# Keep-warm matmuls around TensorE's second modulation slab, and the first parts of x ahead of weight casts, in a two-block transformer kernel

## The reference, cut to what matters

```python
cs = silu(c)                              # c: 1 x 1024
mod = cs @ w_ada[l] + b_ada[l]            # w_ada: 1024 x 6144
sh_a, sc_a, gt_a, sh_f, sc_f, gt_f = split(mod, 6)
h = rms_norm(x, g_mix[l]) * (1 + sc_a) + sh_a
u = h @ w_in[l]                           # w_in: 1024 x 9728
rq, rk, rv, rg, aq, ak, av, ga, gb = split(u, pts)
```

## Time and profile before

| | us |
|---|---|
| median of 3 executions | 1921.5 (1921.12 to 1921.51) |
| span of the profiled execution | 1919.6 |
| TensorE busy | 1826.0 (95%) |
| VectorE busy | 785.6 (41%) |
| ScalarE busy | 570.1 (30%) |
| mean DMA rate | 309 GB/s |

### The profile page before, as it was taken

How to read it: one execution, slowest core, us unless ns; L and a number is a source line. 1 busy time by engine, 2 the same in 40 slices (tenths; PEclk the granted TensorE clock), 3 DMA queues, 4 the chain that set the end, 5 groups by cost and what they waited for, 6 DMA issues and landing times. The chain is left out here.

```text
span 1919.6 us, 24342 instructions
## 1 busy us (share of the span) xinstructions
PE 1826.0 (95%) x9814; PEld 1167.5 (61%) x9814; DVE 785.6 (41%) x1150; ACT 570.1 (30%) x911; POOL 17.0 (1%) x33
## 2 busy tenths in 40 slices
PE   7999999999999999999999999999999999999998
PEld 6799888743333333333333333337888888878886
DVE  6867655411111111111111111115676656666665
ACT  4444554310101000001010010004555544545552
POOL 1000001000000000000000000000000000000000
PEclk7999999999999999999999999999999999999999
DMA  9976756599999999999999999997456646336552
GB/s 343 323 251 230 243 176 217 208 429 428 431 431 430 430 430 431 429 432 431 429 431 431 431 430 430 430 420 233 132 176 197 187 165 219 111 110 198 184 178 99
DMA packets 155400, 592.36 MB, mean 309 GB/s; under 512 B 6703, under 2 KB 85743, under 8 KB 128832
## 3 DMA queue, kind: packets, MB, share of 16 engines
q1 hardware_dynamic: 152816, 582.90, 77.3%
q0 software_dynamic: 2512, 8.45, 1.4%
HBM read 590.26 MB, written 1.07 MB: 308 GB/s over the span
## 5 line engine op out<-in xcount | busy, mean ns | idle before, releaser
L1674 PE MATMUL psum<-shared,expert_arena 128*64 128x512 f32 x1536 | 341.5, 596 | 23.0 <-DMA shared<-in_w_mlp_dram 23.0
L1533 DVE TENSOR_SCALAR expert_arena<-psum 128x512 f32<-128x512 f32 x32 | 22.1, 692 | 583.7 <-PE psum L1674 583.7
L1674 PEld LDWEIGHTS psum<-shared,expert_arena 128*64 128x64 f32 x1536 | 105.5, 137 | 242.5 <-issue 198.8
L415 PE MATMUL psum<-layer_x_parts,layer_w_hi 128*128 128x512 f32 x704 | 240.5, 396 | 0.4 <-DVE layer_x_parts L2144 0.4
L1439 ACT ACTIVATE expert_arena<-expert_arena 128x512 f32<-128x512 f32 x32 | 20.1, 629 | 562.5 <-DVE expert_arena L1533 562.5
L414 PE MATMUL psum<-layer_x_parts,layer_w_lo 128*128 128x256 f32 x616 | 171.8, 279 | 0.0
L352 DVE TENSOR_TENSOR mixer_w_lo<-mixer_ring,mixer_w_hi 128x1024 fp32r<-128x1024 f32 x96 | 116.4, 1223 | 96.7 <-ACT mixer_w_hi L347 96.4
L352 DVE TENSOR_TENSOR layer_w_lo<-slots_ahead,layer_w_hi 128x1024 fp32r<-128x1024 f32 x96 | 116.9, 1224 | 94.5 <-ACT layer_w_hi L347 94.5
L347 ACT CAST mixer_w_hi<-mixer_ring 128x1024 fp32r<-128x1024 f32 x96 | 100.0, 1048 | 158.1 <-PE psum L385 94.2
L415 PEld LDWEIGHTS psum<-layer_x_parts,layer_w_hi 128*128 128x128 f32 x704 | 125.8, 188 | 24.6 <-DVE layer_x_parts L2144 0.8
L383 PE MATMUL psum<-layer_w_hi,layer_x_parts 128*128 128x512 f32 (+1 forms) x384 | 138.7, 361 | 0.4 <-DVE layer_x_parts L2144 0.4
(11 more groups left out here) (311 smaller groups left out, 2683.0 us busy)
## 6 DMA issues: line engine op xcount, KB each, us to landing
shared<-in_w_mlp_dram SPq DMA_DIRECT2D x98, 2048.0 KB, 22.0
expert_ring<-in_w_mlp_dram SPq DMA_DIRECT2D x64, 2048.0 KB, 25.4
mixer_ring<-in_w_in_dram SPq DMA_DIRECT2D x38, 1024.0 KB, 6.3
slots_ahead<-in_w_mlp_dram SPq DMA_DIRECT2D x15, 2048.0 KB, 25.7
mixer_ring<-in_w_ada_dram SPq DMA_DIRECT2D x22, 1024.0 KB, 6.2
slots_ahead<-in_w_ffn_in_dram SPq DMA_DIRECT2D x21, 1024.0 KB, 4.9
memory_kv<-in_w_mlp_dram SPq DMA_DIRECT2D x15, 1024.0 KB, 24.7
kept<-in_w_mlp_dram SPq DMA_DIRECT2D x15, 1024.0 KB, 26.7
```

The source lines that it names most:

```text
L415: last = self.nc.tensor.matmul(out, hi, both[:, k].rearrange("p h s -> p (h s)"), start=k == 0, stop=k == KC - 1)
L1533: nc.vector.tensor_scalar(glu, both[:, :, 0], LIMIT, None, ALU.min).then_inc(glu_ready, 1)
L1674: last = nc.tensor.matmul(U[CAP * h:CAP * h + CAP, N * n:N * n + N], xg[:, k, j, :], expert_slot(M, k // 2)[:, at:at + N], start=False, st ...
```

## The change

TensorE gets keep-warm matmuls: 7 after the scale's slab and before it waits for the shift's slab, one more ahead of columns 2 and 5 of that slab, and 5 between `col1` and `col0a`. ScalarE computes the high parts 0 and 1 of h before the cast of unit 1 (so far after it). VectorE no longer splits unit 0 before `col0a`: it does so within it, after the values 0 and 1, and then forms the low parts 0 and 1, the values 2 and 3, their low parts and unit 1's.

```diff
+            def first_highs(part):
+                act.wait_ge(freed_by_act, jobs.by_name["nT11"].freed)
+                act.wait_ge(scale_ready, 1)
+                wait_freed(act, "col0a" if part[0] < 4 else "col0b")
+                for k in part:
+                    nc.scalar.activation(xh[:, k, :], nT[:, k, :], ACT.Identity, bias=shift[:, k:k + 1], scale=scale[:, k:k + 1]).then_inc(hx_high, 1)
                 if what == "split":
+                    if job == 1:
+                        first_highs(range(2))
                     stream.split_high(act, job)
...
                     if name in ("col0a", "col0b"):
-                        act.wait_ge(freed_by_act, jobs.by_name["nT11"].freed)
-                        act.wait_ge(scale_ready, 1)
-                        wait_freed(act, name)
-                        for k in range(4) if name == "col0a" else range(4, KC):
-                            nc.scalar.activation(xh[:, k, :], nT[:, k, :], ACT.Identity, bias=shift[:, k:k + 1], scale=scale[:, k:k + 1]).then_inc(hx_high, 1)
+                        first_highs(range(2, 4) if name == "col0a" else range(4, KC))
...
                     if job == 0:
                         scale_out()
-                    if job != 1:
+                    if job > 1:
                         stream.split_low(dve, job)
...
-                    for k in [*part, None]:
...
-                        if low >= part[0]:
...
+                    for k in part:
+                        value(k)
+                        if k % 4 == 1 and name == "col0a":
+                            stream.split_low(dve, 0)
+                            low_part(0)
+                            low_part(1)
+                        elif k > part[0] and k % 4 != 2 or name == "col0b" and k % 4 == 2:
+                            low_part(k - 1)
+                    low_part(part[-1])
                     if name == "col0a":
                         stream.split_low(dve, 1)
...
+                        if g == 0:
+                            keep_busy(nc, M, spare, 7)
                         stream.wait_here(pe, job.slots[0])
...
                         for k in range(KC):
+                            if g == 0 and k % 3 == 2:
+                                keep_busy(nc, M, spare, 1)
...
                     g = int(name[3])
+                    if name == "col0a":
+                        keep_busy(nc, M, spare, 5)
                     pe.wait_ge(stream.taken, ada_last[g])
```

More of the change, by code:

```diff
@@ L944, in _, with value, low_part @@
                     wait_freed(dve, "nT11")
-                    for k in [*part, None]:
-                        if k is not None:
-                            nc.vector.tensor_scalar(hT[:, k, :], nT[:, k, :], scale[:, k:k + 1], shift[:, k:k + 1], ALU.mult, ALU.add).then_inc(h_value, 1)
-                        low = part[-1] if k is None else k - 1
-                        if low >= part[0]:
-                            dve.wait_ge(h_value, low + 1)
-                            dve.wait_ge(hx_high, low + 1)
-                            nc.vector.tensor_tensor(xl[:, low, :], hT[:, low, :], xh[:, low, :].bitcast(FP32), ALU.subtract).then_inc(hx_low, 1)
+                    def value(k):
+                        nc.vector.tensor_scalar(hT[:, k, :], nT[:, k, :], scale[:, k:k + 1], shift[:, k:k + 1], ALU.mult, ALU.add).then_inc(h_value, 1)
+                    def low_part(k):
+                        dve.wait_ge(h_value, k + 1)
+                        dve.wait_ge(hx_high, k + 1)
+                        nc.vector.tensor_tensor(xl[:, k, :], hT[:, k, :], xh[:, k, :].bitcast(FP32), ALU.subtract).then_inc(hx_low, 1)
+                    for k in part:
[7 more added lines that the diff above has]
+                    low_part(part[-1])
                     if name == "col0a":
```

## The result

The changed kernel is slower. Median of 6 executions 1929.13 us (1923.88 to 1931.62) against 1921.48 (1921.12 to 1923.92) for 6 of the kernel before; ratio 1.0032, 95% interval 1.0021 to 1.0042.

The account below looks back on a forecast made before the run. The start was taken as bound by col0a, VectorE's chain, POOL's tables and the w_ada slab up to unit 12. Gain 2.01 - 1.14 = 0.87; 1919.6 - 0.87 = 1918.7, plus 1.9 gives 1920.6 us; range 1918.6 to 1925.3.

Parts of the forecast that it names:

- C: TensorE, shift's slab and col1: the clock falls again among one-column matmuls; 1925.3 or 1929.5 us; chance 0.18.
- Step (1): TensorE, seven keep-warm matmuls from 20.0: clock back after 1.5 us, so the shift's slab starts at 23.92.
- Steps (2) and (3): TensorE: slab at full clock to 28.55, col1 to 30.42, five keep-warm to 32.68, addition at 33.67; gain 2.01 us.
- Step (4): VectorE's chain: unit 0's low part now stands inside it, 1.14 us lost, leaving 0.87 of the gain.
- Step (5): ScalarE: two high parts before unit 1's cast stay hidden behind VectorE's work and cost nothing.
- The path to unit 12: From col0a through VectorE's chain, POOL's tables, the w_ada slab's landing and VectorE again: only 0.87 us survives at unit 12.
- rival B: DMA: the landings don't move at all, so the chain's 0.87 us is lost too; 1921.5 us; chance 0.12.
- Rival A: The w_ada slab's landing doesn't hold VectorE, so TensorE's 2.7 us at unit 2 stay; 1918.8 us; chance 0.17.

Follow-up runs that it names:

- cold-start variant: Changed against the kernel before: col1 ahead of the shift's slab, new order, many keep-warm matmuls in both slabs, none ahead of the transposes; 1927.55 us, ratio 1.0027.
- late_tables: The kernel before with POOL's three bias table loads issued only after unit 39's low part; 1920.5 us against 1921.85, ratio 0.9993.
- no_five: The changed kernel without the five keep-warm matmuls between col1 and col0a; 1925.79 us, ratio 1.001 against the kernel before.
- col1_only: The kernel before with col1 run ahead of the shift's slab, POOL's tables early as before; 1920.98 us against 1922.22, ratio 0.9995.

## Why the prediction was wrong

The forecast was 1920.6 within 1918.6 to 1925.3; it came out at 1929.1. The case on the other side, C, was named, with 1925.3 or 1929.5 as its times, and given 0.18.

In short, the step that failed is the cost of the keep-warm matmuls: forecast at a clock that comes back after 1.5 us and then holds, they and the one-column matmuls around them ran mostly at the half clock, and the first shift addition came at 42.99 instead of 33.67.

**Step (1) failed first.** "I take 1.5 us, a quarter of that" priced the seven at 3.92 us from 20.0. The profile has 6.0 us from 22.67. Two things are in it. The 1.5 us were too short by themselves: in the five other profiles with the seven, whose first slab was fast, they took 4.6 to 4.8 us. And I had taken the first slab's full clock as given, as the change doesn't touch it. It is not given: of the eleven profiled kernels whose transposes have no keep-warm matmul in front (both originals among them, with the cold-start variant left out), five show about 6.8 us for it and six 3.7 to 3.9. The Trainium skill ("TensorE: Matmul & The Clock Gate", Part 1) says that the number of slow matmuls at a kernel's start differs from run to run; the traces agree, by 3.1 us for this slab. One profiled execution could not show it, and three equal times hid it: in the kernel before an idle gap lies behind this slab, and where it was slow there (`late_tables`) nothing was lost.

**Steps (2) and (3) failed by the same assumption,** a clock that holds through one-column matmuls. Laid end to end against 42.99: start 2.67 later than I had it, the seven 2.07 more, the slab 0.72, `col1` 1.54, the five 2.15, `col0a` 0.17, together 9.3 us after 33.67. The five are the largest mistake in the change itself: 4.4 us on the path in front of `col0a`. C's mechanism was right: in all six profiles with the seven the clock fell again within the second slab or `col1` (27.4 to 32.0). Its chance was too low. That its 1929.5 lies so near 1929.1 is in part luck: C had the clock fall as the slab begins, 4.2 us dearer than forecast for the slab, where the profile lost 0.72 there and 4.7 before it, in step (1), which C had left alone. The rows had already shown the clock falling among one-column matmuls with the engine busy, and nothing showed it held by a few others between them.

**Step (4) was right:** 1.14 forecast, 1.05 measured in the chain.

**Step (5) was right:** no delay by ScalarE's new order shows beyond the 1.05 of step (4), and in the total the order alone has no measurable cost.

**The path to unit 12 was right, its elasticity wrong.** I let the slab's landing move with POOL's issue. It does so when the chain is late: in the changed kernel VectorE got it 8.6 us after its issue at 53.87, as before. Where the chain came 0.92 us earlier (`no_five`), the slab still landed at about 54.2, 9.6 us after its issue, and at 54.0 in `col1_only`, so 0.87 would have shrunk to nothing: rival B, given 0.12. Why an earlier issue doesn't help stays open. And "45.50 + 8.6 meets 54.12 to the hundredth" said more than its rows: the landing is known to 0.1 us, and VectorE had no idle time ahead of that take. Rival A needs the tables out of the way, and then it works in part (unit 12 at 72.37). The rule of the Trainium skill on alternating queues ("DMA: Bandwidth & Descriptors", Queues, rings and completion order) is not borne out by 46 to 48 here. Later in the same trace it agrees: from 50 to 51 SP's queue q1 and POOL's q0 had about half each.

```profile
q1 hardware_dynamic: 41, 0.17, 51.5%
q0 software_dynamic: 42, 0.17, 48.9%
```

Moving the tables away shortened the landing from 8.6 to 5.2 us, so they did delay the slab.

## What to carry to other kernels

A keep-warm matmul is only free in idle time; on the path here it mostly cost twice its full-clock price, since it stood where the clock was down. Before building on a clock that a profile shows, ask whether it is the same in every execution: look at several, and look for work whose length varies behind an idle gap. And moving real work into the gap (`col1`) shortened the path by 0.8 us at the first shift addition (34.87 against 35.68), where filling the gap with empty work lengthened it.

## What the runs showed of the hardware that was not expected

The same instructions with the same data, 32 one-column records, took about 3.7 us in one profiled execution and 6.8 in another, in kernels that did not differ up to there, and 5.9 once behind three keep-warm matmuls. TensorE busy without a gap for 18.4 us, with keep-warm matmuls among one-column records, had a clock of 0.50 throughout. PEclk reads 1.00 up to the first change on record, and in `late_tables` it reads 1.00 from 24 to 36, where the slab and the sums (6.99 and 6.96 us for 32 records each) ran at half. And the clock fell in the experts' routing in five of the sixteen profiles, for 10 us in one (376.7 to 386.9) and 3 to 4 in the others, not in that of before; whether this is a part of the few microseconds by which executions of one kernel differ is not shown.
